# A GpSimd subtraction of 128x1024 issued as four of 128x256, in a three-layer sequence model on one core

## The chip, the core and the metric

The kernel runs as one program on one core of a Trainium2 chip. The metric is the device time of a run in microseconds (us). Five engines matter: TensorE (PE, with its weight load PEld), VectorE (DVE), ScalarE (ACT), GpSimd (POOL) and SyncE (SP), which issues the loads.

## What is computed

The reference takes `x` (512 tokens by 1024 channels) through two layers of a first block and one layer of a second block. In a layer of the first block the normalised and modulated input is multiplied by `w_in` (some 7,400 columns: queries, keys and values of a gated delta rule, its gate, queries, keys and values of a sliding-window attention, two merging gates). The two mixers' outputs go through `w_dn_out` and `w_swa_out`, are merged and go through `w_o`. Then comes a gated feed-forward part with `w_up` (1024 by 5632) and `w_down` (2816 by 1024). The second block has a band attention and a state-space mixer around the same kind of products:

```python
h = rms_norm(x, norm_mix[l]) * (1.0 + sc1) + sh1
proj = h @ w_in[l]
...
x = x + gt1 * (merged @ w_o[l])
h = rms_norm(x, norm_ffn[l]) * (1.0 + sc2) + sh2
up_act, up_lin = jnp.split(h @ w_up[l], 2, axis=-1)
x = x + gt2 * ((jax.nn.silu(up_act) * up_lin) @ w_down[l])
```

All of it is in float32.

## The kernel before

**A product in three passes.** A float32 weight is split in two: a high part, rounded to the type float32r, and a low part, the rest. So is each activation. A tile of 128 output channels is a *part*. For each of its k blocks of 128 rows, TensorE runs three matmuls of 128x512: high weight by high activation, high by low, low by high (`gemm`, L262 to L279). A part of 8 blocks is 24 matmuls, one of 7 blocks 21, one of 4 blocks 12.

**The pipeline of the weights.** SyncE loads a *slab* (256 output channels, two parts, up to 1 MB) into one of the two places of `ring`. For each part ScalarE copies the slab's half to the high weights (`make_high`, L218; L579 for the gate columns, which are loaded by the part). GpSimd subtracts that high part from the raw slab and so makes the low weights (`make_low`, L220 to L223; L587 for the gates). There are two places for the split weights (`halves(pt, nk)`, by the part's number modulo 2), so `make_high` of part p waits until TensorE has finished part p - 2 (`part_made`). `make_low` waits for `high_made` of its own part, and `gemm` for `low_made`. SyncE waits for `low_made` of both parts of a slab before it loads over it (L526 to L533, L2353). `stage_high` and `stage_low` (L251 to L260) run this two parts ahead, in loops for the feed-forward stages. Each engine has its own queue, strictly in the order in which the code issues.

```python
def make_low(eng, on, n, e, pt, nk=KD, i=0, per=0):
    eng.wait_ge(high_made, pt + 1 + i * per)
    on.tensor_tensor(halves(pt, nk)[1], slot(n, nk)[:, :, e * P:(e + 1) * P], halves(pt, nk)[0], ALU.subtract
                     ).then_inc(low_made, 1)
```

The operands are 128 partitions by nk blocks by 128 columns. With nk = 8 that is 128x1024, with nk = 7 (some parts of `w_down`) 128x896, with nk = 4 (some parts of the second block) 128x512.

**What else GpSimd does.** In the stage of the attention's queries and keys it multiplies by a cosine table (L977, 128x512, ten times in each layer), in one queue with `make_low`: part j + 2's low weights, then L977 of part j. It splits two parts of another place (L416, twice in all), and clears a few small tiles.

**What VectorE does beside it.** In the attention of the first block: masks, maxima, softmax sums (L1109 to L1136) and a causal convolution of each part (L1154, L1157). In the delta rule: triangular solves in small steps (L1755, L1760). For the next stage's modulation vector it accumulates `w_ada` rows (`add_first`, L360 and L363, beside the feed-forward stages of layer 0; L488 and L491 beside the delta rule). In the feed-forward stages: convolution (L2116, L2119), product with the gate (L2127), low activations (L2131). Before the second block it normalises (L2924) and makes low activations (L2928); in it, it makes the state-space model's coefficients in chains of small steps (L2933 to L2975) and in large ones (L2991 to L3016, up to 128x2304), which TensorE waits for at L2578 and L2567. L2031 and L2046 make low activations of the delta rule's outputs and of the merged branches.

Of the kernel before, what the change touches and what calls it, by code (L numbers as in the profile page):

```python
# [11 lines left out]
ALU = mybir.AluOpType  # L12
# [4 lines left out]
P = 128  # L17
D, T, DEPTH = 1024, 512, 2
KD, TT = D // P, T // P
# [90 lines left out]
G_TM, G_SW, G_QKV, G_SO, G_GB, G_GA, G_Z, G_DN, G_WO, G_UP, G_DOWN = 0, 2, 12, 36, 44, 52, 60, 68, 76, 84, 128  # L110
# [22 lines left out]
def build(nc, d, out):  # L133
# [4 lines left out]
    with ExitStack() as ctx:  # L138
# [53 lines left out]
        def slot(n, k=KD, w=256):  # L192

            return ring[:, n % RING, 0:k * w].rearrange("p (k c) -> p k c", k=k)

        def halves(pt, nk, w=P):

            a = SPLIT_W + 4 * (pt % 2)
            return [split[:, a + 2 * n:a + 2 * n + 2, :].rearrange("p a c -> p (a c)")[:, 0:nk * w].rearrange(
                "p (k c) -> p k c", k=nk) for n in range(2)]  # L200

        def products(early, landed, high_made, low_made, part_made, evacuated, bank, use):

            def make_high(act, n, e, pt, nk=KD, i=0, step=0, per=0):

                if e == 0:
                    if n < RING:
                        act.wait_ge(early[n], 16)
                    else:
                        act.wait_ge(landed[n % RING], 16 * (n // RING) + i * (16 * step // RING))
                if pt + per * i >= 2:
                    act.wait_ge(part_made, pt - 1 + i * per)
                nc.scalar.activation(halves(pt, nk)[0], slot(n, nk)[:, :, e * P:(e + 1) * P], ACT.Copy).then_inc(high_made, 1)  # L218

            def make_low(eng, on, n, e, pt, nk=KD, i=0, per=0):  # L220
                eng.wait_ge(high_made, pt + 1 + i * per)
                on.tensor_tensor(halves(pt, nk)[1], slot(n, nk)[:, :, e * P:(e + 1) * P], halves(pt, nk)[0], ALU.subtract  # L222
                                 ).then_inc(low_made, 1)  # L223

            def run_ahead(make, first, count, pt0, work, nk, rounds, loop, started, ahead):

                def one(t, i):
                    k = nk if isinstance(nk, int) else nk[t // 2 % len(nk)]  # L230
                    make(first + t // 2, t % 2, pt0 + t, k, i, count)

                def body(i, last):
                    for t in range(count):
                        if t + 2 < count:
                            one(t + 2, i)
                        elif not last:
                            one(t + 2 - count, i + 1)
                        elif ahead is not None:
                            make(ahead, t + 2 - count, pt0 + count * (rounds - 1) + t + 2, KD, 0, 0)  # L240
                        work(t, i)

                if not started:
                    one(0, 0)
                    one(1, 0)
                if rounds > 1:
                    for i in range(rounds - 1):
                        body(i, False)
                body(rounds - 1, True)

            def stage_high(act, first, count, pt0, work, nk=KD, rounds=1, started=False, ahead=None):  # L251
                def make(n, e, pt, k, i, per):
                    make_high(act, n, e, pt, k, i, per // 2, per)

                run_ahead(make, first, count, pt0, work, nk, rounds, act.Fori, started, ahead)

            def stage_low(eng, on, first, count, pt0, nk=KD, rounds=1, started=False, ahead=None):
                def make(n, e, pt, k, i, per):
                    make_low(eng, on, n, e, pt, k, i, per)

                run_ahead(make, first, count, pt0, lambda t, i: None, nk, rounds, eng.Fori, started, ahead)

            def gemm(pe, gt, rhs, nk=KD, i=0, per=0, weights=None, m=P, k0=0, k1=None, ready=None):

                k1 = nk if k1 is None else k1
                if k0 == 0:
                    pe.wait_ge(low_made, gt + 1 + i * per)
                    if use[gt] > 0:
                        pe.wait_ge(evacuated[bank[gt]], use[gt] + i * (per // BANKS))
                w_high, w_low = weights or halves(gt, nk)  # L270
                for k in range(k0, k1):
                    if ready is not None:
                        pe.wait_ge(ready, k + 1)
                    for w, r in ((w_high, rhs[0]), (w_high, rhs[1]), (w_low, rhs[0])):
                        ins = nc.tensor.matmul(ps[bank[gt]][0:m, :], w[:, k, :], r[:, k, :],  # L275
                                               start=(k == 0 and w is w_high and r is rhs[0]),
                                               stop=(k == nk - 1 and w is w_low))
                if k1 == nk:
                    ins.then_inc(part_made, 1)  # L279

            def by_token(bank, whole, n=P):

                for t in range(TT):
                    ins = nc.tensor.transpose(bank[:, n * t:n * t + n], whole[:, t * P:(t + 1) * P], ident[0:n, 0:n])
                return ins

            return make_high, make_low, stage_high, stage_low, gemm, by_token

        def lasting(name):
# [16 lines left out]
        with ExitStack() as st:  # L306
            sems, layer_sems = {}, []

            def sem(name):

                if name not in sems:
                    sems[name] = st.enter_context(nc.semaphore(name))
                    layer_sems.append(sems[name].num)
                return sems[name]
# [145 lines left out]
            high_made, low_made = sem("high_made"), sem("low_made")  # L460
# [17 lines left out]
            def quarter(n, k):  # L478

                return ring[:, n // 2, 1024 * (n % 2):1024 * (n % 2) + 1024].rearrange("p (k c) -> p k c", k=k)  # L480
# [88 lines left out]
            def slab_of(gt):  # L569

                return SW + (gt - G_SW) // 2 if gt < G_GB else Z + (gt - G_Z) // 2
# [11 lines left out]
            def low(pool, gt):  # L583

                if G_GB <= gt < G_Z:
                    pool.wait_ge(high_made, gt + 1)
                    nc.gpsimd.tensor_tensor(halves(gt, KD)[1], quarter((gt - G_GB) % 2, KD), halves(gt, KD)[0], ALU.subtract  # L587
                                            ).then_inc(low_made, 1)
                else:
                    make_low(pool, nc.gpsimd, slab_of(gt), gt % 2, gt)  # L590

# [184 lines left out]
            for l in range(DEPTH):  # L776
# [16 lines left out]
                with nc.Block() as block:  # L793
# [238 lines left out]
                    @block.gpsimd  # L1032
                    def _(pool):
                        nc.gpsimd.memset(zeros, 0.0).then_inc(zeroed, 1)
                        for t in range(2, QKV_TILES + 2):
                            low(pool, G_QKV + t)
# [192 lines left out]
                    @block.gpsimd  # L1229
                    def _(pool):  # L1230
                        for t in range(2, KD + 2):
                            low(pool, G_SO + t)
# [161 lines left out]
                    @block.gpsimd  # L1394
                    def _(pool):
                        for t in range(2, NT + 2):
                            low(pool, G_GB + t)
# [933 lines left out]
        with ExitStack() as st:  # L2331
# [4 lines left out]
            high_made, low_made, part_made = sem("high_made"), sem("low_made"), sem("part_made")  # L2336
# [853 lines left out]
```

## Time and profile before

| | |
|---|---|
| median of 3 runs | 2728.2 us (2726.16 to 2732.29) |
| span of the profiled execution, first to last instruction | 2719.1 us |
| instructions | 33373 |
| mean granted TensorE clock, as a share of full speed | 0.979 |
| GpSimd's subtractions for low weights | 340 at L222, 32 at L587 |

The profiled execution's own time is not given apart from its span; the median lies 9.1 us above the span. An engine's busy time is the union of its instructions. "Idle before, releaser" is the time for which an engine had nothing to run before an instruction, and what ended it.

### The profile page before, as it was taken

To read this page: it belongs to the slowest core of one execution; us is meant where nothing else is said; L and a number is where in the kernel's file an instruction comes from. 1 tells how busy PE (TensorE), PEld (TensorE's weight loads), DVE (VectorE), ACT (ScalarE), POOL (GpSimd) and SP (SyncE) were. 2 spreads that over 40 slices of the span, in tenths; PEclk is the share of its full clock that TensorE was granted. 3 is DMA by queue.
4 is the path that set the end of the run, shared out by engine and by line. 5 is a ranking of instruction groups with operands and counts; after the bars stand their busy time and mean duration, and the time that the engine had idled before them with its cause. 6 is when DMAs were issued, how large, how long until landed. Compare 5 with 4: busy or idle time off the path is not lost. (4 is left out here: it accounts for less than half of the span.)

```text
span 2719.1 us, 33373 instructions
## 1 busy us (share of the span) xinstructions
PE 2542.2 (93%) x13185; PEld 2041.0 (75%) x13185; DVE 1449.3 (53%) x2548; ACT 1076.4 (40%) x1872; POOL 915.3 (34%) x400
## 2 busy tenths in 40 slices
PE   5989899999989999989998999999999997999998
PEld 3767768897867888866676777877788886786787
DVE  6299748654645546645984562264444206736323
ACT  3345464235332232233554533533333223336432
POOL 1532232112434444434222221243444443322343
PEclk8999999999999999999999999999999999999999
DMA  7222325643333436532223152322222324831232
GB/s 250 69 63 63 125 70 152 197 133 130 101 106 132 140 102 213 200 101 77 63 86 101 42 141 67 136 80 91 93 93 93 104 90 140 150 105 44 70 124 78
DMA packets 331391, 300.00 MB, mean 110 GB/s; under 512 B 56719, under 2 KB 302821, under 8 KB 330213
## 3 DMA queue, kind: packets, MB, share of 16 engines
q1 hardware_dynamic: 279268, 279.52, 33.0%
q10 hardware_dynamic: 51968, 18.35, 2.6%
q8 instruction: 105, 1.72, 0.3%
q14 instruction: 50, 0.40, 0.0%
HBM read 267.92 MB, written 29.93 MB: 110 GB/s over the span
## 5 line engine op out<-in xcount | busy, mean ns | idle before, releaser
L275 PE MATMUL ps<-hh,split 128*128 128x512 f32 x3808 | 1286.2, 405 | 28.3 <-POOL split L222 17.6
L222 POOL TENSOR_TENSOR split<-ring,split 128x1024 fp32r<-128x1024 f32 (+2 forms) x340 | 808.0, 2378 | 1370.1 <-ACT split L218 1334.4
L275 PEld LDWEIGHTS ps<-hh,split 128*128 128x128 f32 x3808 | 724.4, 190 | 200.1 <-POOL split L222 31.7
L275 PE MATMUL ps<-hl,split 128*128 128x512 f32 x1904 | 749.5, 394 | 0.0
L218 ACT ACTIVATE split<-ring 128x1024 fp32r<-128x1024 f32 (+1 forms) x336 | 341.6, 1018 | 870.1 <-PE ps L275 674.9
L275 PEld LDWEIGHTS ps<-hl,split 128*128 128x128 f32 x1904 | 363.5, 191 | 73.0 <-issue 8.4
L275 PE MATMUL ps<-split 128*128 128x512 f32 x1152 | 281.5, 401 | 8.9 <-DVE split L1136 7.1
L275 PEld LDWEIGHTS ps<-split 128*128 128x128 f32 x1152 | 215.9, 188 | 69.6 <-issue 14.4
L2269 PE MATMUL ps<-split 128*128 128x512 f32 x1056 | 242.9, 391 | 0.0
L2269 PEld LDWEIGHTS ps<-split 128*128 128x128 f32 x1056 | 199.0, 189 | 41.3
L587 POOL TENSOR_TENSOR split<-ring,split 128x1024 fp32r<-128x1024 f32 x32 | 76.2, 2382 | 311.3 <-ACT split L579 311.3
L2127 DVE TENSOR_TENSOR wk<-wk,ps 128x512 f32<-128x512 f32 x44 | 30.3, 688 | 180.6 <-PE ps L275 180.6
L1157 DVE SCALAR_TENSOR_TENSOR big<-ps,pv,big 128x511 f32<-128x511 f32 x144 | 107.8, 749 | 5.1
L1175 ACT ACTIVATE big<-big 128x256 f32<-128x256 f32 (+1 forms) x88 | 41.5, 473 | 95.0 <-DVE big L1119 95.0
L2305 DVE SCALAR_TENSOR_TENSOR x<-ps,mod,x 128x512 f32<-128x512 f32 x16 | 12.0, 749 | 123.6 <-PE ps L2269 123.6
L363 DVE SCALAR_TENSOR_TENSOR kd<-spare,c_act,kd 128x512 f32<-128x512 f32 x56 | 61.3, 1095 | 26.3 <-DMA spare<-in_w_ada_dram 24.5
L2131 DVE TENSOR_TENSOR split<-wk,split 128x512 fp32r<-128x512 f32 x44 | 71.2, 1619 | 5.6 <-ACT split L2163 5.6
L2116 DVE TENSOR_SCALAR wk<-ps,pv 128x512 f32<-128x512 f32 x44 | 33.0, 749 | 76.9 <-PE ps L275 70.3
L1284 DVE TENSOR_TENSOR big<-big,wk 128x512 f32<-128x512 f32 x32 | 39.0, 1219 | 62.0 <-ACT wk L1266 62.0
L2119 DVE SCALAR_TENSOR_TENSOR wk<-ps,pv,wk 128x511 f32<-128x511 f32 x88 | 65.9, 749 | 3.1
L491 DVE SCALAR_TENSOR_TENSOR vs<-ring,c_act,vs 128x256 f32<-128x256 f32 x112 | 63.7, 569 | 1.5 <-DMA ring<-in_w_ada_dram 0.4
L956 DVE SCALAR_TENSOR_TENSOR wk<-ps,pv,wk 128x512 f32<-128x512 f32 x20 | 15.0, 751 | 90.0 <-ACT wk L890 90.0
(426 smaller groups left out, 3226.3 us busy)
## 6 DMA issues: line engine op xcount, KB each, us to landing
ring<-in_w_in_dram SPq DMA_DIRECT2D x60, 1024.0 KB, 5.2
ring<-in_w_up_dram SPq DMA_DIRECT2D x44, 1024.0 KB, 5.1
ring<-in_w_in_dram SPq DMA_DIRECT2D x34, 512.0 KB, 5.1
big<-in_w_ada_dram SPq DMA_DIRECT2D x16, 1024.0 KB, 8.7
ring<-in_w_ada_dram SPq DMA_DIRECT2D x32, 512.0 KB, 3.7
spare<-in_w_ada_dram SPq DMA_DIRECT2D x16, 1024.0 KB, 7.4
ring<-in_w_down_dram SPq DMA_DIRECT2D x16, 896.0 KB, 5.1
ring<-in_w_swa_out_dram SPq DMA_DIRECT2D x8, 1024.0 KB, 5.2
```

The costliest lines, as they stand in the source:

```text
L218: nc.scalar.activation(halves(pt, nk)[0], slot(n, nk)[:, :, e * P:(e + 1) * P], ACT.Copy).then_inc(high_made, 1)
L222: on.tensor_tensor(halves(pt, nk)[1], slot(n, nk)[:, :, e * P:(e + 1) * P], halves(pt, nk)[0], ALU.subtract).then_inc(low_made, 1)
L275: ins = nc.tensor.matmul(ps[bank[gt]][0:m, :], w[:, k, :], r[:, k, :], start=(k == 0 and w is w_high and r is rhs[0]), stop=(k == nk - 1 a ...
L363: nc.vector.scalar_tensor_tensor(out=acc, in0=w, scalar=c_act[:, k:k + 1], in1=acc, op0=ALU.mult, op1=ALU.add).then_inc(first_added, 1)
L491: nc.vector.scalar_tensor_tensor(out=acc, in0=w, scalar=c_act[:, k:k + 1], in1=acc, op0=ALU.mult, op1=ALU.add).then_inc(ada_added, 1)
L587: nc.gpsimd.tensor_tensor(halves(gt, KD)[1], quarter((gt - G_GB) % 2, KD), halves(gt, KD)[0], ALU.subtract).then_inc(low_made, 1)
L1157: nc.vector.scalar_tensor_tensor(out=y[:, s:], in0=tile[:, 0:T - s], scalar=w[3 - s], in1=y[:, s:], op0=ALU.mult, op1=ALU.add).then_inc(c_ ...
L1175: nc.scalar.activation(half, half, ACT.Exp, bias=st_(u, 2)[:, j:j + 1], accum_out=st_(u, 3)[:, j:j + 1]).then_inc(a_exp, 1)
L1284: nc.vector.tensor_tensor(tile, tile, wk[:, 10 + n % 2, :], ALU.mult).then_inc(n_scaled, 1)
L2119: nc.vector.scalar_tensor_tensor(out=y[:, s:], in0=ps_[:, 0:T - s], scalar=w[2 - s], in1=y[:, s:], op0=ALU.mult, op1=ALU.add).then_inc(u_t ...
L2131: nc.vector.tensor_tensor(g_low[:, ds(j + 4 * i, 1), :], wk[:, 8 + j % 4, :].unsqueeze(1), g_high[:, ds(j + 4 * i, 1), :], ALU.subtract).t ...
L2269: ins = nc.tensor.matmul(ps[bank[gt]][:, :], w[:, k, :], r[:, k0 + k, :], start=(k0 + k == 0 and w is w_high and r is g_high), stop=(k0 + ...
```

## The change

Each subtraction for low weights becomes one instruction for every two blocks: four of 128x256 for 8 blocks, three of 128x256 and one of 128x128 for 7, two of 128x256 for 4. The wait stands before the first, the increment of `low_made` on the last. The elements, the places and the order are as before. L416 and L977 stay.

```diff
 def make_low(eng, on, n, e, pt, nk=KD, i=0, per=0):
     eng.wait_ge(high_made, pt + 1 + i * per)
-    on.tensor_tensor(halves(pt, nk)[1], slot(n, nk)[:, :, e * P:(e + 1) * P], halves(pt, nk)[0], ALU.subtract
-                     ).then_inc(low_made, 1)
+    raw = slot(n, nk)[:, :, e * P:(e + 1) * P]
+    for k in range(0, nk, 2):
+        ks = slice(k, min(k + 2, nk))
+        ins = on.tensor_tensor(halves(pt, nk)[1][:, ks, :], raw[:, ks, :], halves(pt, nk)[0][:, ks, :], ALU.subtract)
+    ins.then_inc(low_made, 1)
...
     if G_GB <= gt < G_Z:
         pool.wait_ge(high_made, gt + 1)
-        nc.gpsimd.tensor_tensor(halves(gt, KD)[1], quarter((gt - G_GB) % 2, KD), halves(gt, KD)[0], ALU.subtract
-                                ).then_inc(low_made, 1)
+        raw = quarter((gt - G_GB) % 2, KD)
+        for k in range(0, KD, 2):
+            ks = slice(k, k + 2)
+            ins = nc.gpsimd.tensor_tensor(halves(gt, KD)[1][:, ks, :], raw[:, ks, :], halves(gt, KD)[0][:, ks, :],
+                                          ALU.subtract)
+        ins.then_inc(low_made, 1)
```

## Rows read from the trace of the kernel before

**Rows 1.** The page, busy time and share of each engine.

```profile
PE 2542.2 (93%) x13185; PEld 2041.0 (75%) x13185; DVE 1449.3 (53%) x2548; ACT 1076.4 (40%) x1872; POOL 915.3 (34%) x400
```

**Rows 2.** Timeline in the feed-forward stage: start us, us, instruction, idle before and releaser.

```profile
1007.50 1.06 ACT L218 ACTIVATE split<-ring 128x1024 fp32r<-128x1024 f32 x1 [2.42 <-PE ps L275]
...
1008.64 2.40 POOL L222 TENSOR_TENSOR split<-ring,split 128x1024 fp32r<-128x1024 f32 x1 [3.09 <-ACT split L218]
...
1012.88 1.07 ACT L218 ACTIVATE split<-ring 128x1024 fp32r<-128x1024 f32 x1 [3.80 <-PE ps L275]
...
1014.03 2.48 POOL L222 TENSOR_TENSOR split<-ring,split 128x1024 fp32r<-128x1024 f32 x1 [2.98 <-ACT split L218]
...
1014.50 2.55 DVE L2131 TENSOR_TENSOR split<-wk,split 128x512 fp32r<-128x512 f32 x1 [0.26 <-ACT split L2163]
```

**Rows 3.** Waits: who waited for whom, us in total, times, longest us.

```profile
PEld ps L275 <- POOL split L222: 36.5, 23, 4.3
```

**Rows 4.** Timeline of GpSimd from 150 us, beside the attention of layer 0.

```profile
150.75 2.38 POOL L222 TENSOR_TENSOR split<-ring,split 128x1024 fp32r<-128x1024 f32 x1 [7.22 <-ACT split L218]
159.19 4.72 POOL L222 TENSOR_TENSOR split<-ring,split 128x1024 fp32r<-128x1024 f32 x2 [6.06 <-ACT split L218]
```

**Rows 5.** Groups of GpSimd by form: xcount, busy us, mean ns, idle before and releasers.

```profile
L222 POOL TENSOR_TENSOR split<-ring,split 128x1024 fp32r<-128x1024 f32 x284 | 707.2, 2492 | 1231.9 <-ACT split L218 1196.3 <-DVE hl L917 35.6
...
L222 POOL TENSOR_TENSOR split<-ring,split 128x896 fp32r<-128x896 f32 x32 | 69.3, 2164 | 89.0 <-ACT split L218 89.0
L222 POOL TENSOR_TENSOR split<-ring,split 128x512 fp32r<-128x512 f32 x24 | 31.6, 1316 | 49.1 <-ACT split L218 49.1
```

**Rows 6.** Timeline of GpSimd from 80 us, the stage of attention queries and keys.

```profile
101.79 1.29 POOL L977 TENSOR_TENSOR wk<-wk,cos_t 128x512 f32<-128x512 f32 x1 [3.17 <-DVE wk L956]
103.04 2.85 POOL L222 TENSOR_TENSOR split<-ring,split 128x1024 fp32r<-128x1024 f32 x1
```

**Rows 7.** Timeline of TensorE from 102 us, the same stage.

```profile
106.39 0.79 PE L275 MATMUL ps<-hh,split 128*128 128x512 f32 x1
```

**Rows 8.** Timeline of GpSimd at the start of the second block.

```profile
2265.47 5.26 POOL L222 TENSOR_TENSOR split<-ring,split 128x1024 fp32r<-128x1024 f32 x2 [13.77 <-ACT split L218]
2284.69 4.70 POOL L222 TENSOR_TENSOR split<-ring,split 128x1024 fp32r<-128x1024 f32 x2 [13.97 <-ACT split L218]
```

**Rows 9.** Timeline of VectorE beside the first pair of rows 8.

```profile
2266.89 1.64 DVE L2928 TENSOR_TENSOR hl<-b_scaled,hh 128x512 fp32r<-128x512 f32 x1 [1.12 <-ACT hh L2746]
2268.45 2.83 DVE L2924 SCALAR_TENSOR_TENSOR b_scaled<-x,pv,wk 128x512 f32<-128x512 f32 x1
```

**Rows 10.** Timeline of VectorE from 2284 us.

```profile
2284.74 2.33 DVE L2964 TENSOR_TENSOR vs<-vs 128x16 f32<-128x16 f32 x1
2287.10 2.32 DVE L2965 TENSOR_TENSOR vs<-vs 128x16 f32<-128x16 f32 x1
...
2308.78 4.64 DVE L2992 TENSOR_TENSOR b_read_tmp<-b_tile,vs 128x2304 f32<-128x2304 f32 x1
2313.46 2.56 DVE L2993 TENSOR_TENSOR b_read_w<-b_read_w,b_read_tmp 128x2304 f32<-128x2304 f32 x1
```

**Rows 11.** Timeline of GpSimd from 2290 us.

```profile
2313.77 4.50 POOL L222 TENSOR_TENSOR split<-ring,split 128x1024 fp32r<-128x1024 f32 x1 [2.76 <-ACT split L218]
```

**Rows 12.** Timeline of GpSimd from 2640 us.

```profile
2654.36 5.38 POOL L222 TENSOR_TENSOR split<-ring,split 128x1024 fp32r<-128x1024 f32 x2 [2.24 <-ACT split L218]
```

**Rows 13.** Timeline of TensorE from 2320 us.

```profile
2337.13 1.11 PE L2567 MATMUL ps<-cst,x 128*128 128x128 f32 x4 [4.47 <-DVEq L3030]
```

**Rows 14.** Line L363: duration ns min/median/max, first and last start us, forms.

```profile
L363 DVE SCALAR_TENSOR_TENSOR kd<-spare,c_act,kd x56: 750/752/2910, 1040.3 to 1159.5; 128x512 f32<-128x512 f32 x56
```

**Rows 15.** Line L2031: the same columns, and who waited for it (us, times).

```profile
L2031 DVE TENSOR_TENSOR split<-big,split x16: 677/1582/2486, 662.3 to 1800.9; 128x512 fp32r<-128x512 f32 x16
...
  PE ps L275: 1.2, 2
```

**Rows 16.** Line L491: duration ns min/median/max, first and last start us, forms.

```profile
L491 DVE SCALAR_TENSOR_TENSOR vs<-ring,c_act,vs x112: 464/477/2647, 410.8 to 626.4; 128x256 f32<-128x256 f32 x112
```

## The prediction

> **What bounds the kernel now.** I began with the busy shares of the page. TensorE works for 93% of the span, GpSimd for 34% [rows 1]. A longer GpSimd instruction therefore costs nothing by itself: it costs where TensorE stands and waits for low weights, or where it would begin to.
>
> So the timeline of the steady stretch comes next. In the feed-forward stage ScalarE's copy starts when TensorE ends a part, at 1007.50 and 1012.88: a part lasts some 5.4 us. GpSimd's subtraction follows from 1008.64 to 1011.04, and TensorE wants it at about 1012.8 [rows 2]. That leaves some 1.6 us of cover after the wake-up of its wait. The reader is to see that the chain copy, subtraction, next part is tied to TensorE's last part but one, so this cover is there afresh each time, and does not run out.
>
> The waits view then says where there is no cover: TensorE's weight load waited 23 times for L222, 36.5 us in total [rows 3]. I went through GpSimd's timeline beside TensorE's starts. With L587 and the start of the second block, 18 subtractions of 128x1024 (or nearly) and 5 of 128x512 end some 0.05 us before the matmul that wants them. The first of the large ones is at 150.75, then 159.19 [rows 4], the last at 2654.36 [rows 12]. The two longest of the 23 waits, 4.3 us each, are not among them: there ScalarE ends last.
>
> The last view is VectorE beside GpSimd. L2131 starts at 1014.50 while GpSimd works (1014.03 to 1016.51), and ends at 1017.05, 0.54 us behind it [rows 2]. The two engines shut each other out when both read two operands of SBUF. Four pieces instead of one change who waits for whom, so both engines must be costed.
>
> **The fixed time of three more instructions.** The same elements are handled; what is added is what an instruction costs beside its elements. 128x512 takes 1.29 us [rows 6], 128x1024 2.38 [rows 4]: 2 x 1.29 - 2.38 = 0.20 us fixed. In a queue the next starts 1.25 us after a start, 0.04 before the end [rows 6], so a further piece costs 0.16, and three of them **0.48 us**. From below, the fixed parts could overlap wholly: 0. From above, 0.20 each and the scatter of these rows: 0.7. I take 0.48, because the form is the same and 256 lies next to 512. The 128x896 form also becomes four pieces, the 128x512 form two (0.16) [rows 5].
>
> The Trainium skill, "GPSIMD Engine Reference", section "Instruction dispatch", gives the software dispatch as one indirect call of tens of cycles at 1.2 GHz. Fifty cycles would be an estimated 0.04 us, 0.12 for three, and the next sum would be 18 x 0.12 = 2 us by it instead of 8.6; no row isolates the dispatch.
>
> Exposed subtractions: 18 x 0.48 = 8.6, 5 x 0.16 = 0.8, together **+9.4 us**.
>
> In the stage of attention queries and keys, GpSimd does L977, then the low weights at once, 103.04 to 105.89 [rows 6], and TensorE begins at 106.39 [rows 7]: 0.45 us of cover after the wake-up, against 0.48. Of the 8 such parts of each layer the first has only 0.1 and loses 0.4; the others lose 0 to 0.1. Together **+1.2** (bounds 0 and 16 x 0.48 = 8). Everywhere else the 1.2 to 2.4 us of cover hide 0.48; without it, the other 330 would cost 160 us. SyncE's loads wait for `low_made` and start 0.5 us later, but the slab is wanted some two parts later: nothing, apart from a load or two that already land last.
>
> **VectorE between the pieces.** Two queued subtractions took 5.26 us at 2265.47 [rows 8] where the pair at 159.19 took 4.72 [rows 4]. L2928 waited for the first and ended at 2268.53, and L2924 then waited until 2271.28 [rows 9]. So VectorE gets in at a boundary between two GpSimd instructions, and an operation of 128x512 costs GpSimd about 0.5 there. There will be three boundaries more in each subtraction. At that very pair, which TensorE waits for, five more such operations get in: +2.5. At the pair of 2284.69 [rows 8] VectorE has a string of steps of 0.17 us, of which only one got through before (2284.74, 2287.10) [rows 10], and the triangular solves beside L587 are alike: some four exposed subtractions with three steps of 0.2, +2.0. In the last stages another +1.8. Together **+6.3** (bounds 0 and 15).
>
> Where VectorE streams L363 (0.75 us each, two operands) beside `w_down` in layer 0 [rows 14], a subtraction grows by 0.48 + 3 x 0.45 = 1.8 us over a cover of some 1.3: some 8 of them lose 0.5, **+4** (0 to 9).
>
> VectorE's large operations, 2.56 us each, stretch a subtraction already: 4.50 us at 2313.77 [rows 11], with L2993 in front [rows 10]. With four pieces three more of them can get in. But TensorE waits for VectorE at 2337.13 all the same, 4.47 us [rows 13], and a delay before that point comes out of this wait. I take **+2** (0 to 20).
>
> **What VectorE gains.** Its blocked operations wait 0.7 us at most instead of 2.4. This counts only where VectorE holds TensorE up. L2031 lasts up to 2.49 us instead of 0.68, and TensorE waited twice for it, 1.2 us [rows 15]: -1.2. L491, blocked for 2.65 instead of 0.48 [rows 16], stands before some short waits of TensorE in the delta rule: -2. Beside the attention, blocked softmax steps and L2046: -1.8. Together **-5** (bounds 0 and -10).
>
> **Sum:** 9.4 + 1.2 + 6.3 + 4 + 2 - 5 = +17.9 us. Against the profiled execution's span that is 2719.1 to 2737.0. The median of the runs lies 9.1 us above that span, so 2728.2 becomes **2746 us**.
>
> **Rivals.** *GpSimd keeps the port through its four pieces.* The next piece is queued already, and VectorE might not win the boundary. For it: 0.04 us of overlap leaves no visible gap [rows 6]. Against it: rows 9. Only the fixed time counts: 9.4 + 1.2 = +10.6, 2739 us.
>
> *VectorE's large operations get in at each boundary and the wait at 2337.13 does not absorb it.* A subtraction in that stretch would last 4 x 0.7 + 3 x 2.56 = 10.5 us against the 5.4 of a part, and two or three in a row would cost TensorE some 5 us each and the chain behind as much: 18 + 15 = +33, 2761 us. For it: rows 10 and 11. Against it: the 4.47 us of rows 13, and that VectorE's chain sets that stage.
>
> *Not slower: VectorE's relief outweighs the surcharges.* The place is the 18 exposed subtractions against the waits set by VectorE. If the pieces overlap and a further one costs 0.05 instead of 0.16, the exposed ones cost 18 x 0.15 = 2.7; if few VectorE operations use the boundaries where TensorE waits (+3) and the relief is at its bound (-10), the sum is -4, 2724 us. It decides from where relief exceeds both surcharges; at 0.16 it can't, since 9.4 + 6.3 is over 10. For it: a blocked step of 2.3 us where 0.17 would do [rows 10]. Against it: the two forms of rows 5, whose means say 2 x 1316 - 2492 = 0.14 us even with the blocked ones in. The Trainium skill, same page and section, says that each GpSimd core starts instruction N+1 as soon as it has finished its share of N, which would favour such an overlap; the 0.04 us of rows 6 show little of it.
>
> *Nothing to measure:* the exposed waits are refunded by later ones, 2728 to 2732.
>
> **How the numbers follow.** This kernel can be told from no change from about 0.2%, 5.5 us. My forecast has 0.46 (own range 2736 to 2758), the kept port 0.20, the large operations 0.14: slower 0.80. Not slower has 0.12, of it 0.08 faster, nothing to measure 0.08: same 0.12, faster 0.08. The range goes from 2727, which leaves out only the faster end, to 2764, which takes in most of the third case.
>
> **What would show it.** Pieces of 128x256 of 0.7 to 0.75 us at L224 to L226, starting some 0.7 apart when nobody interferes; GpSimd's busy time up by 372 x 0.48, some 170 us; VectorE's total down, with L2131's longest well under 2.55; the wait at the first exposed subtraction (151 us) longer by 0.5, the pair of 2265.47 by 3; L977's stage longer by about 0.6 in each layer. I am wrong if the pieces start 0.6 us apart or less, if no VectorE operation ends between two pieces, or if the stretch from 2295 to 2337 moves by more than 5 us.

## The result

The changed kernel is slower, by less than half of what was forecast: 2736.09 us, median of 14 runs (2729.79 to 2746.08), against 2729.55 for 14 runs of the kernel before. The ratio is 1.0028, 95% interval 1.0017 to 1.0039, or +7.6 us (+4.6 to +10.6); the forecast was +17.9.

**Two parts of the time.** The span of a run times its mean granted TensorE clock is the time that it would last if the whole of it ran at the upper level, 2.4 GHz. The rest of the span is what the clock costs (a little too much, since some of the slow time falls into waits). I call them *stalls and work* and *clock*. The first scatters by only some 2 us from run to run, so it tells small changes apart (± is one standard error of the mean):

| mean over the runs, us | stalls and work | clock | mean clock |
|---|---|---|---|
| before (93 runs beside the experiments) | 2661.6 | 66.1 | 0.9758 |
| after (14 runs) | 2659.9 ± 0.5 | 75.6 ± 1.4 | 0.9724 |
| difference | -1.7 | +9.5 | |

So all stalls that the pieces add and all that they remove come out nearly even, and what is measured is a lower clock. The prediction has no term for that. The split has a limit: among the 93 runs of the kernel before, a microsecond more at the clock goes with only 0.7 of span, so part of it is taken off the other column again. By that slope the 9.5 are worth an estimated 6.8 us of time, and stalls and work +1 instead of -1.7. The clock part of the kernel before also differs between the four chips on which its 93 runs were taken, from 64.9 to 67.7; 75.6 lies well above all of them. Each experiment is set against the runs of its own chip.

### The profile page after: what moved, and what is told of

The parts are those of the page before. It is cut to its first block and busy times, and to the rows that moved or that the text cites. A ratio compares the mean times of both kernels' runs of the same rounds, so it can differ in the third digit from the quotient of the medians.

```text
span 2731.9 us, 34441 instructions
## 1 busy us (share of the span) xinstructions
PE 2558.1 (94%) x13185; PEld 2048.6 (75%) x13185; DVE 1307.4 (48%) x2548; ACT 1077.4 (39%) x1872; POOL 1152.7 (42%) x1468
## 5 line engine op out<-in xcount | busy, mean ns | idle before, releaser
L225 POOL TENSOR_TENSOR split<-ring,split 128x256 fp32r<-128x256 f32 (+1 forms) x1312 | 1027.3, 814 | 1174.8 <-ACT split L218 1139.1
L278 PE MATMUL ps<-split 128*128 128x512 f32 x1152 | 283.5, 404 | 7.1 <-DVE split L1143 7.1
L2276 PE MATMUL ps<-split 128*128 128x512 f32 x1056 | 247.7, 396 | 1.6 <-POOL split L225 1.6
L593 POOL TENSOR_TENSOR split<-ring,split 128x256 fp32r<-128x256 f32 x128 | 94.3, 768 | 291.3 <-ACT split L582 291.3
L366 DVE SCALAR_TENSOR_TENSOR kd<-spare,c_act,kd 128x512 f32<-128x512 f32 x56 | 52.8, 943 | 37.7 <-DMA spare<-in_w_ada_dram 35.8
L1291 DVE TENSOR_TENSOR big<-big,wk 128x512 f32<-128x512 f32 x32 | 23.6, 738 | 78.2 <-ACT wk L1273 78.2
L494 DVE SCALAR_TENSOR_TENSOR vs<-ring,c_act,vs 128x256 f32<-128x256 f32 x112 | 57.4, 513 | 1.5 <-DMA ring<-in_w_ada_dram 0.3
L1161 DVE TENSOR_SCALAR big<-ps,pv 128x512 f32<-128x512 f32 x48 | 35.9, 747 | 45.1 <-PE ps L278 45.1
```

The costliest lines, as they stand in the source:

```text
L225: ins = on.tensor_tensor(halves(pt, nk)[1][:, ks, :], raw[:, ks, :], halves(pt, nk)[0][:, ks, :], ALU.subtract)
L366: nc.vector.scalar_tensor_tensor(out=acc, in0=w, scalar=c_act[:, k:k + 1], in1=acc, op0=ALU.mult, op1=ALU.add).then_inc(first_added, 1)
L494: nc.vector.scalar_tensor_tensor(out=acc, in0=w, scalar=c_act[:, k:k + 1], in1=acc, op0=ALU.mult, op1=ALU.add).then_inc(ada_added, 1)
L593: ins = nc.gpsimd.tensor_tensor(halves(gt, KD)[1][:, ks, :], raw[:, ks, :], halves(gt, KD)[0][:, ks, :], ALU.subtract)
L1161: nc.vector.tensor_scalar(y, tile[:, :], w[3], None, ALU.mult).then_inc(c_tap, 1)
L2276: ins = nc.tensor.matmul(ps[bank[gt]][:, :], w[:, k, :], r[:, k0 + k, :], start=(k0 + k == 0 and w is w_high and r is g_high), stop=(k0 + ...
```

## The profile after

The page, busy times, and GpSimd's groups by form (times, total us, mean ns, idle before):

```profile
PE 2558.1 (94%) x13185; PEld 2048.6 (75%) x13185; DVE 1307.4 (48%) x2548; ACT 1077.4 (39%) x1872; POOL 1152.7 (42%) x1468
```

```profile
L225 POOL TENSOR_TENSOR split<-ring,split 128x256 fp32r<-128x256 f32 x1280 | 1009.9, 820 | 1174.8 <-ACT split L218 1139.1 <-DVE hl L924 35.7
L593 POOL TENSOR_TENSOR split<-ring,split 128x256 fp32r<-128x256 f32 x128 | 94.3, 768 | 291.3 <-ACT split L582 291.3
...
L225 POOL TENSOR_TENSOR split<-ring,split 128x128 fp32r<-128x128 f32 x32 | 18.7, 586 | 0.0
```

Beside [rows 1], GpSimd works 237 us longer (the prediction's sign was some 170; its 372 x 0.48 makes 179, and the rest is what VectorE's operations add) and VectorE 142 us shorter. L222 and L587 of before are L225 and L593 here, later lines are up by 7; the experiments' lines are up by 13 to 19.

The steady stretch, GpSimd and then VectorE (start us, us, number of instructions in the row), to be laid beside [rows 2]:

```profile
1010.75 2.82 POOL L225 TENSOR_TENSOR split<-ring,split 128x256 fp32r<-128x256 f32 x4 [2.67 <-ACT split L218]
...
1015.67 0.68 DVE L2138 TENSOR_TENSOR split<-wk,split 128x512 fp32r<-128x512 f32 x1
1016.61 0.89 DVE L2138 TENSOR_TENSOR split<-wk,split 128x512 fp32r<-128x512 f32 x1 [0.26 <-ACT split L2170]
```

Four pieces last 2.82 us where one instruction took 2.40: 0.42 more, with nobody between. And L2138 does not last until the subtraction's end any more: 0.89 us where it was 2.55.

TensorE's waits (us in total, times, longest), to be laid beside [rows 3]. L2559 is the start of the second block, L1083 the attention.

```profile
PEld ps L278 <- POOL split L225: 53.4, 54, 4.8
...
PEld ps L2559 <- POOL split L225: 13.2, 1, 13.2
PE ps L2559 <- POOL split L225: 12.4, 1, 12.4
...
PE ps L1083 <- DVE split L1143: 23.6, 14, 3.6
```

The same view of the kernel before:

```profile
PE ps L1076 <- DVE split L1136: 27.1, 16, 3.6
...
PE ps L2552 <- POOL split L222: 9.3, 1, 9.3
```

Where TensorE waits for GpSimd it waits longer (12.4 us at the start of the second block, where it was 9.3). Where it waits for VectorE in the attention it waits less (23.6 us where it was 27.1).

## Where in the second block

GpSimd from 2266 us. The pair at 2266.23 answers to the first of [rows 8]; a row of x8 is two subtractions:

```profile
2266.23 8.35 POOL L225 TENSOR_TENSOR split<-ring,split 128x256 fp32r<-128x256 f32 x8 [13.35 <-ACT split L218]
...
2299.85 15.00 POOL L225 TENSOR_TENSOR split<-ring,split 128x256 fp32r<-128x256 f32 x8 [5.90 <-ACT split L218]
2320.78 9.75 POOL L225 TENSOR_TENSOR split<-ring,split 128x256 fp32r<-128x256 f32 x8 [5.92 <-ACT split L218]
```

VectorE in the coefficient stretch (compare [rows 10, 11]):

```profile
2299.20 2.56 DVE L3000 TENSOR_TENSOR b_read_w<-b_read_w,b_read_tmp 128x2304 f32<-128x2304 f32 x1
2301.80 2.98 DVE L2998 TENSOR_TENSOR b_read_w<-b_tile,vs 128x2304 f32<-128x2304 f32 x1
2304.81 2.97 DVE L2999 TENSOR_TENSOR b_read_tmp<-b_tile,vs 128x2304 f32<-128x2304 f32 x1
2307.82 2.96 DVE L3000 TENSOR_TENSOR b_read_w<-b_read_w,b_read_tmp 128x2304 f32<-128x2304 f32 x1
```

The two engines take turns at each boundary. An operation of 2.56 us loses 0.42 to a piece; a piece of 0.7 us loses some 2.3 to the operation (pieces start at 2302.32, 2305.33 and 2308.33 here, and each lasts 3.04 us). Eight pieces take 15.0 us where eight unhindered ones would take 5.6. TensorE pays:

```profile
2311.41 0.79 PE L278 MATMUL ps<-hh,split 128*128 128x512 f32 x1 [3.93 <-POOL split L225]
...
2312.43 1.05 PE L278 MATMUL ps<-hh,split 128*128 128x512 f32 x2
...
2316.86 0.40 PE L278 MATMUL ps<-hl,split 128*128 128x512 f32 x1
2317.10 0.62 PE L278 MATMUL ps<-hh,split 128*128 128x512 f32 x2
...
2327.81 0.50 PE L278 MATMUL ps<-hh,split 128*128 128x512 f32 x1 [2.83 <-POOL split L225]
```

Two waits are new, 3.93 and 2.83 us (the kernel before had one of 0.29 in this stretch; one of 1.07 follows at 2354.91). In exchange the wait of 4.47 us for L3030 [rows 13] is gone, since VectorE now finishes its coefficients in time. About the first new wait TensorE runs at half speed for a while: two matmuls take 1.05 us, and 0.62 from 2317.10 on. The windows view shows it (stretch, length, busy us of each engine, granted clock, DMA share, GB/s). Each stretch starts and ends at the same matmuls in both kernels. The kernel before:

```profile
2270.78:2287.09 16.31, 13.36 (x48) 10.55 (x49) 15.12 (x42) 9.21 (x17) 2.40 (x2) 0.85 0.61 146
2287.09:2304.04 16.95, 16.95 (x67) 12.70 (x68) 16.18 (x24) 5.26 (x8) 9.01 (x3) 1.00 0.18 62
2304.04:2340.17 36.13, 30.44 (x188) 24.93 (x187) 34.46 (x26) 7.24 (x9) 14.71 (x5) 0.96 0.80 169
```

The changed kernel:

```profile
2274.64:2291.24 16.60, 13.22 (x48) 10.42 (x48) 14.86 (x54) 7.34 (x15) 2.82 (x5) 0.87 0.42 122
2291.24:2316.27 25.03, 21.10 (x67) 15.42 (x68) 24.44 (x19) 5.26 (x8) 17.72 (x12) 0.80 0.14 44
2316.27:2347.98 31.71, 28.88 (x189) 23.68 (x187) 16.79 (x16) 7.24 (x9) 15.51 (x17) 1.00 0.79 159
```

The middle stretch lasts 8.1 us longer. 5.0 of them are its clock, 0.80 where it was 1.00. The last one is 4.4 us shorter, which is the refund. In this trace the stall is paid for twice, once as a wait and once in slow matmuls about it. But one trace does not show that the pieces lower the clock. In the trace of the last experiment but one, where the second block has one instruction each time as before, the same matmuls have a granted clock of 0.80, 0.85 and 0.95. Its middle stretch:

```profile
2298.99:2318.74 19.75, 19.75 (x68) 14.75 (x68) 19.06 (x22) 5.26 (x8) 8.97 (x3) 0.85 0.16 53
```

What the pieces do to the clock must be read from many runs.

## The experiments

Each has four pieces (three and one, or two, for the shorter forms) where a condition holds, and one instruction elsewhere; the rest is the kernel before.

```diff
+def blocks_of(layer, pt, nk):
+    four = <condition>
+    return 2 if four else nk
...
-    for k in range(0, nk, 2):
-        ks = slice(k, min(k + 2, nk))
+    step = blocks_of(LAYER[0], pt, nk)
+    for k in range(0, nk, step):
+        ks = slice(k, min(k + step, nk))
```

### One part of the change at a time

Conditions: `layer < DEPTH and G_QKV + 2 <= pt < G_UP + 2` (attention, delta rule, merge); `layer < DEPTH and pt >= G_DOWN + 2`; `layer == DEPTH`.

> Four pieces only for the parts whose products run beside the mixers of the first block (from the third part of queries, keys and values to the second of w_up), both layers; one instruction everywhere else. Theory A, VectorE's relief is larger than I priced and lies here: the changed kernel had gained 2.6 us by 336 us, some 3 in the delta rule, 4 and 4 more in layer 1, with losses between: this kernel is 4 to 10 us faster than before, ratio 0.996 to 0.999. Rival B, those gains are only the scatter of one execution (clock, landings) and the relief is the 5 us I forecast, eaten by some 10 exposed subtractions of 0.48: within 2 us of before.

2721.34 us, ratio 0.9967 [0.995, 0.9984]: -9 us, as Theory A had it.

> Four pieces only for the parts of w_down, both layers. Theory A, with VectorE streaming L363 beside them in layer 0 each subtraction takes VectorE's operations in at its boundaries and outgrows its cover: +4 to +6 us (the changed kernel lost 5.8 between 1030 and 1160 us), nothing in layer 1, where no such stream runs. Rival B, the cover of 1.3 us holds: within 1 us.

2728.66 us, ratio 1.0003 [0.9992, 1.0013]: +0.8 us, below Theory A.

> Four pieces only in the second block. Theory A: +3 to +4 at its first two subtractions, which VectorE's operations are let into, +10 from the subtraction of 2300 us that lets three of 2.3 to 2.6 us in, -6 back at the wait for VectorE at 2337, +2 in the last stages: +9 to +12, with a subtraction of 10 us or more in the profile. Rival B, the fixed time alone: 6 exposed subtractions of 0.48 and five small ones: +4.

2740.06 us (5 runs), ratio 1.0049 [1.0037, 1.0062]: +13.4 us (+10.1 to +16.9), on Theory A's side; the fixed time alone (+4) is excluded. TensorE's waits for GpSimd there are 12.4, 3.4, 2.2 and 3.7 us.

Split as above, against 2662.2 and 64.9 of their own kernel before:

| | stalls and work | clock |
|---|---|---|
| mixers only | -11.6 | +3.1 |
| `w_down` only | +1.7 | -0.9 |
| second block only | +6.0 | +7.5 |
| sum | -3.9 | +9.7 |
| the whole change | -1.7 | +9.5 |

The parts add up within their scatter of some 2 us. The change is two changes of opposite sign. The second block's clock rested on 5 runs, hence the last experiment below.

### Two pieces instead of four

`return nk // 2`, and 4 + 3 blocks for 7.

> Two pieces of 128x512 (4 and 3 blocks where there are 7) instead of four, everywhere. One fixed time of 0.14 to 0.16 and one boundary more instead of three. Theory A, boundaries let VectorE in and that is most of the price: 18 x 0.15 = 2.7 for the fixed time, +1.5 at the start of the second block, +3 in the stretch of large operations less what the wait at 2337 takes back, +1 beside w_down, and more than half of the relief (blocked for 1.3 us at most): -3 to +2 us. Rival B, the price goes with the fixed time and the relief with the pieces alike, a third of the change: +2.5 us.

2723.4 us, 0.9986 [0.9975, 0.9998], or -3.8 us: Theory A's range; the +2.5 of Rival B is excluded. Stalls and work fall by 8.0 us against their own kernel before, the clock part rises by 4.1 (± 1.9). One boundary comes at a third of the fixed time and lets fewer large operations in: TensorE waits 1.1 and 1.4 us in the coefficient stretch instead of 3.9 and 2.8. How much of the 8.0 is gained in the first block and how much is not lost in the second, this run does not tell.

### The attention alone, and the mixers without their exposed subtractions

Conditions: `layer < DEPTH and G_QKV + 2 <= pt < G_SO + 10`; `layer < DEPTH and G_QKV + 4 <= pt < G_UP + 2 and pt not in (G_GB + 5, G_GB + 6)`.

> Four pieces only for the parts whose products run beside the sliding-window attention and its output product, both layers. Theory A, the relief of the softmax steps of VectorE is a large part of the gain of e1: 3 to 5 us faster than before (0.998 to 0.999), the rest of e1's 8.9 us then lies in the delta rule. Rival B, the gain of e1 lies in the delta rule alone (the solves, L491, L2031), and the attention's three exposed subtractions in each layer eat its own: within 1.5 us.

2723.51 us, 0.9977 [0.9967, 0.9987]. Stalls and work fall by 4.2 us (± 0.8), where all of the mixers' parts gave 11.6: the other 7 lie in the delta rule and the merge.

> As e1, but the first two parts beside the attention and two of the gates' parts, whose subtractions TensorE waits for, stay one instruction. Theory A, an exposed subtraction costs 0.43 us more in four pieces, and more with VectorE between: 4 in each layer give 3 to 4 us back, 0.5 to 1 of it lost again because VectorE is blocked longer beside them: 2 to 3 us faster than e1, 0.9955 of before. Rival B, what VectorE gains beside them is worth as much: the same as e1 within 1 us.

2720.85 us, **0.9959 [0.9944, 0.9973]**: the lowest ratio of all, 11 us below the kernel before and by the ratios some 19 below the changed one. It rests on 6 runs, and against the mixers alone the intervals overlap, so what the exposed subtractions cost there is not resolved.

### Where the boundary must lie

The same parts as in the mixers alone, cut 1+1+1+5, 1+7 or 7+1 blocks.

> As e1, but each subtraction is cut into 1, 1, 1 and 5 blocks instead of 2, 2, 2, 2: the same four instructions, elements and three boundaries, but VectorE can be shut out for 1.5 us instead of 0.7. Theory A, what e1 gains is the shorter time for which VectorE is shut out: half or less of the gain remains, 1 to 4 us faster than before. Rival B, it is that VectorE gets in early at all (at the first boundary), or something else in having four: the same as e1, 8 to 9 us faster.

2721.06 us, 0.9965 [0.9951, 0.9979]: by the ratio the same as four even pieces, Rival B. The split says otherwise: stalls and work fall by 6.4 us (± 0.6) and not by 11.6 (± 1.1), which is Theory A's half.

> The mixers' parts of e1, each subtraction as 1 and then 7 blocks: one instruction more, with a boundary after some 0.4 us. In the kernel before, 119 blocked operations of VectorE beside the mixers start on average 0.8 us into the subtraction, a third of them before 0.4 us. Theory A, the relief goes by how long an operation that has come still waits for a boundary: a third to a half of e1's gain, less a fixed time of 0.14 on each exposed one: 2 to 5 us faster than before. Rival B, one early boundary is all it takes: 8 to 10 us faster, as e1 and e8.

2727.22 us, 0.9998 [0.9986, 1.001]; stalls and work +0.8.

> The same with 7 and then 1 block: the same number of instructions and boundaries, but the boundary comes after 2.1 us, when nearly all blocked operations have been waiting for long. Theory A: hardly any relief, 10 exposed subtractions dearer by 0.14: between 1 us faster and 2 us slower than before. Rival B, that the gain of e1 comes from anything but the place of the boundary: as e9.

2722.24 us, 0.9973 [0.9963, 0.9984]; stalls and work -5.1. Theory A expected the reverse order of the last two, Rival B no difference. One spot shows how the place of a boundary counts, VectorE's softmax of a part of the attention with GpSimd beside it. The kernel before:

```profile
182.68 1.43 DVE L1116 TENSOR_TENSOR big<-big,sink 128x2 f32<-128x2 f32 x1
184.14 0.16 DVE L1118 TENSOR_TENSOR big<-sink,big 128x2 f32<-128x2 f32 x1
...
181.70 2.39 POOL L222 TENSOR_TENSOR split<-ring,split 128x1024 fp32r<-128x1024 f32 x1 [9.33 <-ACT split L218]
```

With 1+7:

```profile
181.56 1.56 DVE L1134 TENSOR_TENSOR big<-big,sink 128x2 f32<-128x2 f32 x1
183.16 0.16 DVE L1136 TENSOR_TENSOR big<-sink,big 128x2 f32<-128x2 f32 x1
...
180.58 2.52 POOL L235 TENSOR_TENSOR split<-ring,split 128x128 fp32r<-128x128 f32 x2 [9.31 <-ACT split L227]
```

With 7+1:

```profile
181.14 1.17 DVE L1134 TENSOR_TENSOR big<-big,sink 128x2 f32<-128x2 f32 x1
182.34 0.38 DVE L1136 TENSOR_TENSOR big<-sink,big 128x2 f32<-128x2 f32 x1
...
180.16 2.54 POOL L235 TENSOR_TENSOR split<-ring,split 128x896 fp32r<-128x896 f32 x2 [8.90 <-ACT split L227]
```

With four even pieces:

```profile
181.88 0.48 DVE L1134 TENSOR_TENSOR big<-big,sink 128x2 f32<-128x2 f32 x1
182.40 0.65 DVE L1136 TENSOR_TENSOR big<-sink,big 128x2 f32<-128x2 f32 x1
...
180.91 2.82 POOL L235 TENSOR_TENSOR split<-ring,split 128x256 fp32r<-128x256 f32 x4 [8.67 <-ACT split L227]
```

An operation of 128x2 elements, 0.16 us when free, is stuck for as long as the instruction beside it lasts. It comes 0.98 us after GpSimd's start each time. With 1+7 the boundary has passed by then, and it ends 2.54 us after GpSimd's start (2.41 in the kernel before); with 7+1 it is let in before the last block and ends after 2.15; with even pieces it lasts only 0.48. So a boundary counts if it comes soon after VectorE's operation does. The spot does not account for all of what 7+1 gains: the operation behind it waits for the last block then, and ends 2.56 us after GpSimd's start where it was 2.60 before. TensorE's waits for L1136 (L1154 in these kernels) in the attention rank the versions much as stalls and work do: 29.3 us with 1+7, 27.1 before, 25.5 with 7+1, 25.3 with 1+1+1+5, 23.8 with four even pieces. From 1+7 to 7+1 that is 3.8 of 5.9 us; from before to 7+1 it is 1.6 of 5.1, and the rest was not traced. With 1+7 and 7+1 the rows of these waits are

```profile
PE ps L1094 <- DVE split L1154: 29.3, 18, 3.6
```

```profile
PE ps L1094 <- DVE split L1154: 25.5, 16, 3.6
```

### The second block taken apart

Conditions, with `layer == DEPTH`: `2 <= pt < 16`, `pt < 2`, `pt >= 16`.

> Four pieces only for parts 2 to 15 of the second block, beside VectorE's coefficient chain. Theory A, VectorE's operations of 2.3 to 2.6 us get in at every boundary and two subtractions last 7 to 11 us; after what the wait at the coefficients gives back, +6 to +9 us of e3's 11 to 13. Rival B, the wait at the coefficients (4.5 us) absorbs nearly all of it, and e3's loss lies at its first pair and its end: +1 to +3.

2737.52 us, 1.0023 [1.0011, 1.0035]: +6.0 in stalls and work, +0.9 at the clock. TensorE waits for GpSimd four times (and once 0.57 us, at 2319.36), and not for L3030 and L3009:

```profile
2292.56 0.50 PE L288 MATMUL ps<-hh,split 128*128 128x512 f32 x1 [3.39 <-POOL split L235]
2311.59 0.80 PE L288 MATMUL ps<-hh,split 128*128 128x512 f32 x1 [4.42 <-POOL split L235]
2334.96 0.64 PE L288 MATMUL ps<-hh,split 128*128 128x512 f32 x1 [4.43 <-POOL split L235]
2358.23 0.50 PE L288 MATMUL ps<-hh,split 128*128 128x512 f32 x1 [1.09 <-POOL split L235]
```

The first of them was 2.96 us before. Together they are 10.6 us more than before, and 4.47 and 0.93 (L3009) are refunded: +5.3 in this trace, beside +6.0 over the runs. Two new waits of 4.4 us each, and next to nothing at the clock (+0.9 ± 1.5): that does not bear out that each new wait costs a second time there.

> Four pieces only for the first two parts of the second block, for which TensorE waits. Theory A, VectorE's operations of 0.7 us are let in at up to six boundaries, at 0.45 each, on top of 2 x 0.43: +3 us, of which the profile of e3 shows 3.1. Rival B, only the fixed time: +0.9.

2728.49 us, 0.9999 [0.9989, 1.001]. The wait is 12.42 us here too, 3.1 longer, and no longer time comes of it that the interval (up to +2.7 us) would show. The trace has half of it back 65 us later: TensorE waits neither 0.29 us for GpSimd nor 0.93 for L3009 any more, and 4.14 for L3030 instead of 4.47, 1.55 us in all. The matmul behind that wait starts 64.62 us after the first of the block, where it was 66.35. In the run with one instruction throughout the second block and a slow stretch before (shown above) the wait for L3030 is 4.14 us as well, so a late TensorE seems to get this much back from waits for VectorE whatever made it late. Over the runs stalls and work are 4.5 us lower and the clock part 3.9 higher (± 1.4) than in their own kernel before; that much against each other for one pair of subtractions I cannot explain.

> Four pieces in the second block from its part 16 on (from about 2400 us), one instruction elsewhere. All of the second block in four pieces cost +13.4 us, the coefficient stretch alone +6.3, the first pair alone -0.8. Theory A (the parts of the second block simply add): what is left over, +7 to +8 us, is here, ratio 1.0025 to 1.003; the exposed subtractions from 2400 us on would then cost over 2 us more each than the 0.43 of the fixed time. Theory B (the stages interact: what a change in the first 100 us costs is refunded or not by what follows, and the profiles of the whole second block, where TensorE's idle time grows by only 0.5 us from 2400 to 2530 us and by 1.1 after it, are right): +1.5 to +3 us here, ratio 1.0005 to 1.001, and the pair and the stretch together cost more than each alone.

2734.16 us, 1.0008 [0.9995, 1.0021]: +2.9 in stalls and work, 0.0 (± 2.0) at the clock, as Theory B had it. The three together, by their ratios, are worth +8.2 us (give or take 5.6) against +13.4 of the whole block: the difference is not resolved. At the clock the three make 3.9 + 0.9 + 0.0, against 7.5 (± 2.1) of the whole.

### Everything but the second block

Conditions: `layer < DEPTH`; `layer < DEPTH or pt >= 16`.

> Four pieces in both layers of the first block, one instruction in the second block. Split each run's span into span x mean granted clock and the rest, the time lost to the lower clock. Over all runs the changed kernel has 2659.9 and 75.6 us, the kernel before 2661.6 and 66.1: the stalls are worth -1.6 us in sum, and the clock +9.5. Theory C (stalls: the mixers -11.6, w_down +1.7, the second block +6.0; clock: nearly all of it from the second block, +7.5, where new waits of TensorE of some 3 to 4 us are each followed by a stretch at 1.2 GHz): span x clock falls by 8 to 10 us, the loss at the clock returns to 66 to 69 us, ratio 0.997 to 0.998. Theory D (the clock falls because of the pieces everywhere, by what they do to the rhythm of TensorE or to the engines' load; the second block has no special part in it): the loss at the clock stays at 73 us or more, ratio 0.999 to 1.0005.

2723.99 us, 0.9972 [0.9958, 0.9987]. Stalls and work 2654.2 ± 0.5 against 2662.1, clock 67.4 ± 2.0 against 65.7.

> As the run before it, with four pieces also in the second block from its part 16 on; only the first pair and the coefficient stretch of the second block keep one instruction. Theory C: the late parts added 2.9 us of stalls and nothing at the clock when they were changed alone, so span x clock lies some 3 us above the run before, the loss at the clock is the same within 2 us, ratio 0.998 to 0.999; the first 140 us of the second block then hold the whole difference to the changed kernel, 8 us or so. Theory D: the loss at the clock is 73 us or more here too, and the changed kernel is at most 4 us slower than this one.

2723.73 us, 0.9985 [0.997, 1.0]. Stalls and work 2655.0, clock 68.1 ± 1.7.

Theory C holds in where the clock is lost, Theory D falls. Without the second block's pieces the loss at the clock returns to 67.4 us (75.6 with them), and the clock itself to 0.9752. From the other side the second block is worth 2659.9 - 2654.2 = +5.7 in stalls and work and 75.6 - 67.4 = +8.2 at the clock; alone it was worth +6.0 and +7.5. Most of it stands in its first 140 us: 4.9 and 7.5 (± 2.2) of these. Why the clock falls there is open: Theory C's account, new waits with slow matmuls behind them, fits the trace of the changed kernel, but neither the coefficient stretch alone (+0.9) nor the slow stretch in the trace without the second block's pieces.

## Why the forecast was half right

**The fixed time: right.** 0.48 forecast for three more instructions, 0.42 measured (2.82 against 2.40). It goes by their number: 1+1+1+5 blocks took 2.80 us at 149.90, 1+7 blocks 2.52. The wait at the first exposed subtraction grew by 0.42, from 0.56 to 0.98 us:

```profile
153.18 0.50 PE L275 MATMUL ps<-hh,split 128*128 128x512 f32 x1 [0.56 <-POOL split L222]
```

```profile
153.87 0.50 PE L278 MATMUL ps<-hh,split 128*128 128x512 f32 x1 [0.98 <-POOL split L225]
```

These rows also show that the changed kernel had lost 0.27 us before that wait, where 0.6 was forecast for the stage of attention queries and keys of this layer; traces scatter by more than that up to there, and no run isolates the +1.2 of that stage.

The estimate of 0.12 us from the Trainium skill, "GPSIMD Engine Reference", section "Instruction dispatch", is too low by 0.30; no row says where the rest goes.

**VectorE between the pieces: right at the pair, and in kind.** Forecast +3 there, 9.3 to 12.4 measured. The rival in which GpSimd keeps the port is excluded by VectorE's operations between its pieces (2301.80 to 2310.78). The pair alone moved the time by -0.3 us (-3.0 to +2.7): half of its wait was given back.

**`w_down`: too dear.** +4 forecast, +0.8 measured (-2.2 to +3.5). I counted three boundary operations of 0.45 in each subtraction. With that each lasts 4.2 us. In the trace with four pieces at `w_down` alone the 20 between 1043 and 1170 us last 2.5 to 4.2, 3.3 on average, and only six of them 3.8 or more. L363 waited 38 us for its own loads there, which probably leaves fewer of its operations beside each subtraction than I counted.

**The large operations: the step was wrong as reasoned, and the sign of being wrong that I set for it came up.** I held that a delay before 2337 comes out of the wait for L3030 and took +2 for the stretch. The wait of 4.47 us was indeed paid back, but what took its place is larger: waits of 3.4, 4.4, 4.4, 0.6 and 1.1 us with the stretch alone, where 3.0 and 0.3 were. It cost +6.3 us (+3.0 to +9.6). In the changed kernel the stretch between the matmuls of 2287.09 and 2337.13 grew from 50.0 to 55.2 us, just over the 5 us of that sign. The rival of 33 us overshot, since it did not take the refund into account.

**What VectorE gains: the first step that failed.** It was priced -5 with a bound of -10. The mixers alone took 11.6 us off stalls and work (9 us off the time), with their own surcharges already in. All of the first block gains 7.9 us of stalls and work net; its surcharges in the forecast were some 5 of fixed time in the mixers, 1.2 in the attention queries' stage, 1 beside the solves and 4 at `w_down`. Taking the measured 1.7 for the last, and the forecast for the others, which were not measured, the relief is an estimated -17. I had looked for blocked operations that stand directly before a wait of TensorE, and found L2031 and L491. In the attention the relief comes through a queue instead: each softmax step held up delays all that VectorE has behind it, and the last of them makes what TensorE waits for. The attention alone gave 4.2 us net, and the waits for L1136 fell from 27.1 to 23.8 us; the prediction priced all of that at 1.8 with a neighbour. The larger part, some 7 us in the delta rule and the merge, which the prediction priced at 3.2, was not followed to a wait: that remains open. The rival that held this, "not slower", had the right mechanism and the wrong condition: it thought that relief could not pass 10 us.

**The clock: the second step that failed, a term put at nothing.** +9.5 us in the split (an estimated 6.8 of time), 8 of them from the second block. Here two errors cancel in part: relief is some 12 us larger than forecast, and the clock takes most of it away. That the kernel came out slower at all, as forecast, is luck: the stalls that the forecast sums up come to -1.7 us by the split, or +1 by the slope, where it has +17.9.

**Which engine blocks whom.** The Trainium skill, "SBUF — State Buffer", section "Who interferes with whom", says that the order of issue and not the form of an operation decides who is blocked. The trace agrees: 128x2 elements were stuck 1.27 us behind 128x1024, pieces of 0.7 us behind 128x2304, and 128x2304 in its turn 0.42 us behind a piece of 128x256.

## What to carry to other kernels

In this kernel, cutting an instruction that shares a resource helped the other engine and hurt its own. It paid where TensorE waits for the other, and not where the other's operations are larger still: cut in the mixers and whole in the second block, it was worth 9 to 11 us. Look for relief in the total of the waits that end with the relieved engine's queue, not only in the operations that stand last before one. And split the span of the runs into span times clock and the rest: it showed at once that the slowdown was not in the stalls, and it tells 2 us apart where the medians need 5. Read it with the slope of 0.7 in mind, and take a clock from many runs, not from one trace.

## What was not expected of the hardware

- A small piece is the weaker party: a 128x2304 operation lost 0.42 us at a boundary, the piece of 128x256 beside it 2.3 us; eight pieces took 15.0 us.
- An operation of 128x2 elements took up to 1.43 us beside a subtraction (1.95 with 1+7 blocks) where it takes 0.16 alone.
- Over the runs of the kernel before, each microsecond lost at the clock goes with 0.7 us of span (correlation 0.91 in 93 runs), which is most of the scatter between its runs.
- Open: why the clock is lower with pieces at the start of the second block, where the delta rule gains its 7 us, and why stalls and work fell by 4.5 us in the runs with the first pair alone.
